# A hybrid decoder step: decayed scores over the later halves' columns, and one decayed tile per level in place of two

## The chip, the cores and the metric

The kernel runs on one core of a Trainium2 chip. Time is the device time of one launch in microseconds, the median of several runs. The engines are TensorE (PE, with its weight loads shown as PEld), VectorE (DVE), ScalarE (ACT), GpSimd (POOL) and the queues that move data.

## The reference

Two decoder layers run over 256 prompt tokens and 8 x 8 sample tokens. Each layer adds a mixer and then a feed-forward part (a dense SwiGLU in layer 0, the best two of eight experts in layer 1). The mixer projects to an HGRN2 group (4 heads, keys and values of 128) and a Mamba-2 group. The change touches the HGRN2 group alone:

```python
q, k, v, logf                  # (tokens, 4, 128); logf is the log of the forget gate
S_t = diag(f_t) S_{t-1} + k_t v_t^T          # per head
o_t = S_t^T q_t
# in chunks:
G      = cumsum(logf)
scores[t, s] = sum_k q[t, k] * exp(G[t, k] - G[s, k]) * k_in[s, k]    for s <= t
o_intra = scores @ v
o_inter = (q * exp(G)) @ state
```

The decay differs for each of the 128 components of a key, so the scores are no plain product of queries with keys: exp(G[t] - G[s]) has to be split at a token between s and t.

## The kernel before

**The levels.** The kernel splits a tile of 128 tokens in seven levels (LV = 7; in the tile of 64 sample tokens, sequences of 8, there are three, LS = 3). At level v the tokens are cut into blocks of 2b, b = 2^v, and each block into an earlier and a later half. A pair (s, t) belongs to the one level at which s lies in the earlier and t in the later half of one block, and its decay is split at the middle of that block: M[level v] holds, for every token, the decay between it and the middle of its block. So keys times M and queries times M, multiplied with each other, give the decayed scores of level v. A last level holds the pairs s = t. M is laid out with the 128 components on the partitions and (level, token) on the columns; M[nl] is the decay from the start of the tile.

**Tiles and heads.** TILES holds the tiles 0 and 1 (prompt, 128 tokens) and 2 (sample, 64 tokens); ORDER = (2, 0, 1), so HEADS, the list of pairs (tile, head) that the head loop runs over, has 12 entries per layer: four sample heads, four of the first prompt tile, four of the second. The loop runs once in each layer. Buffers alternate by head: M, Yq, Yk and SC have two copies each.

**The steps of a head.**
- exponents (PE, L1872): logs of the gates times a 0/1 table give the exponents of all levels in PSUM, in four products of 512 columns (two of 256 in the sample tile). ScalarE turns them into M ("decays", L800 and L803).
- products (VectorE, L1229): Yq = M times qT and Yk = M times kT, each one instruction over all levels (L1241, L1251). Between them stand, in the second prompt tile, qGp and egp (L1245, L1246) and, in the sample tile, egl and qG.
- scores (PE, L1887): for the levels 0 to 4 (LOW = 5) one product each of the whole tile, Yk by Yq (L1901); one of kT by qT for s = t (L1904); for the levels 5 and 6 only the blocks that are wanted, 2 + 1 products (L1908), into the columns of the last one. The tile's scores take 6 x 128 columns in two PSUM banks; the sample tile's 4 x 64.
- masked (VectorE, L1253): all of them times a 0/1 table into SC (L1260; L1263 in the sample tile).
- output (PE, L1913): the values (vtk) by each level's part of SC, six products that add up in one PSUM region (L1923; four in the sample tile), and in the second prompt tile one with the state (L1928).

All of it is fp32, and each fp32 product is two records in the trace. In a PE record `128*128 128x64` reads: the weights have 128 rows and 128 columns, the moving operand 128 rows and 64 columns.

**What sets the order.** PE's order is written out by hand at L2103 and below. For head j it issues: exponents of head j + 1; transposes and questions to the states of the sample sequences (turn_said, ask) where it is their turn; output of head j - 1; a piece of the sample's state; transposes of the values where a tile begins; scores of head j; transposes of the keys; the tile's state. At the last head of a tile the output stands ahead of the exponents. VectorE runs products of head j + 1, then masked of head j, then other pieces of the loop: the low half of the weights that come in for the next projection (spL, L1050, 2.3 us each), copies of states (SH), and so on. The engines keep in step by counters: y_done2 (products are ready), sc_mm (scores are in PSUM), sc_done (masked), o_mm (output read SC), x_exp (M is there). Before, scores of head j wait for sc_done of head j - 1, since all heads write the same two banks of scores.

## Time and profile before

| what | value |
|---|---|
| median of 3 runs | 1766.98 us (1762.48 to 1768.28) |
| the profiled execution | 1768.81 us, its span 1767.0 us |
| mean granted PE clock in it | 0.977 of full speed |
| PE busy | 1704.7 us, 96% |
| VectorE busy | 1291.5 us, 73% |
| ScalarE busy | 1039.1 us, 59% |
| GpSimd busy | 98.3 us, 6% |
| chain of work that ended last | PE 92%, DVE 5%, ACT 1%, issue 1% |

The profile is of one execution; its time stands 1.8 us above the median of the runs. Of a PE or VectorE row in a timeline the first number is the start and the second the length, both in us, "x9" says that nine like instructions follow each other, and brackets hold the idle time just before the row and what ended it. In the table of stretches each row is a stretch of the span, its length, then the busy time and, in brackets, the number of instructions of PE, PEld, DVE, ACT and POOL, the granted PE clock (1.00 is 2.4 GHz, 0.50 is 1.2 GHz), the share of the DMA engines and GB/s. Rows of groups give line, engine, operation, tiles, shapes and count, then total busy us and mean ns of one, then the idle time before them.

### The profile page before, as it was taken

Reading aid. Unit: us, or ns where it says so; the run is one execution under the profiler, and the core shown is the slowest. Engines: PE = TensorE matmul, PEld = TensorE weight load, DVE = VectorE, ACT = ScalarE, POOL = GpSimd, SP = SyncE. Lnnn points to the kernel's source line nnn. Section 1 sums busy time; section 2 is a strip of 40 time slices with the busy share of each in tenths; the row PEclk is TensorE's granted clock in tenths of the full one; section 3 lists DMA queues with packets and bytes.
Section 4 is the critical chain, followed back from the end, with each engine's and each line's share of the span. In section 5 each row is a group of like instructions: output and inputs, shape, how many; then the busy total and the mean of one; then the engine's idle time right before and its main releaser. Section 6 shows DMA issues by size and latency. Waiting matters only on the chain.

```text
span 1767.0 us, 23227 instructions
## 1 busy us (share of the span) xinstructions
PE 1704.7 (96%) x9594; PEld 1484.4 (84%) x9594; DVE 1291.5 (73%) x1119; ACT 1039.1 (59%) x942; POOL 98.3 (6%) x85
## 2 busy tenths in 40 slices
PE   8999889999999999789999999999999999899997
PEld 7988778999999978678888888888888888788886
DVE  6636755444357347649988888888888888888897
ACT  4443333333334344257777777777777777777776
POOL 2001120000000011203200000000000000000200
PEclk9997989999999989899999999999999999999999
DMA  9549263443553513259999999999999999899994
GB/s 298 167 149 276 57 180 109 160 141 102 146 168 123 164 39 85 60 179 341 392 394 396 397 366 388 367 387 394 363 386 377 366 398 386 312 394 365 381 393 186
DMA packets 272616, 474.07 MB, mean 268 GB/s; under 512 B 41578, under 2 KB 103266, under 8 KB 272504
## 3 DMA queue, kind: packets, MB, share of 16 engines
q1 hardware_dynamic: 266432, 452.37, 71.9%
q10 hardware_dynamic: 3368, 12.75, 2.2%
q0 software_dynamic: 2704, 7.39, 1.5%
q8 instruction: 78, 1.28, 0.3%
q14 instruction: 34, 0.28, 0.0%
HBM read 454.69 MB, written 29.84 MB: 274 GB/s over the span
## 4 chain that ended last, share of the span: by engine, by line
PE 92%; DVE 5%; ACT 1%; issue 1%; DMA 0%; ACTq 0%; DVEq 0%
PE ps L1712 17%; PE ps L1713 17%; PE ps L2355 12%; PE ps L1707 9%; PE ps L1708 9%; PE ps L2376 6%; PE ps L1806 4%; PE ps L2241 3%; PE ps L1923 2%; PE ps L2259 1%; PE ps L2394 1%; PE ps L1901 1%; PE ps L2203 1%; DVE spL L1592 1%; PE ps L1883 1%
## 5 line engine op out<-in xcount | busy, mean ns | idle before, releaser
L1592 DVE TENSOR_TENSOR spL<-ring,spH 128x2048 fp32r<-128x2048 f32 x336 | 767.3, 2292 | 99.2 <-ACT spH L967 96.5
L967 ACT ACTIVATE spH<-ring 128x2048 fp32r<-128x2048 f32 x336 | 643.0, 1916 | 130.7 <-PE ps L2355 68.1
L1712 PE MATMUL ps<-spH,XH 128*128 128x512 f32 x896 | 353.7, 395 | 1.8 <-issue 1.8
L1713 PE MATMUL ps<-spH,XL 128*128 128x512 f32 x896 | 349.4, 390 | 0.0
L1050 DVE TENSOR_TENSOR spL<-ring,spH 128x2048 fp32r<-128x2048 f32 (+1 forms) x74 | 158.8, 2146 | 182.3 <-ACT spH L662 182.2
L1707 PE MATMUL ps<-hnH,spH 128*128 128x320 f32 x928 | 277.4, 313 | 4.0 <-DVE hnL L1065 2.2
L1708 PE MATMUL ps<-hnL,spH 128*128 128x320 f32 x928 | 275.7, 311 | 0.0
L662 ACT ACTIVATE spH<-ring 128x2048 fp32r<-128x2048 f32 (+1 forms) x74 | 133.4, 1803 | 187.7 <-PE ps L2241 73.6
L2355 PE MATMUL ps<-spL,XH 128*128 128x512 f32 x896 | 240.9, 390 | 2.3 <-issue 1.8
L2355 PEld LDWEIGHTS ps<-spL,XH 128*128 128x128 f32 x896 | 168.0, 188 | 39.0 <-issue 2.2
L1712 PEld LDWEIGHTS ps<-spH,XH 128*128 128x128 f32 x896 | 168.3, 188 | 35.9 <-issue 2.2
L1713 PEld LDWEIGHTS ps<-spH,XL 128*128 128x128 f32 x896 | 168.4, 188 | 33.9
L1707 PEld LDWEIGHTS ps<-hnH,spH 128*128 128x128 f32 x928 | 176.5, 190 | 7.4 <-issue 4.8
L1708 PEld LDWEIGHTS ps<-hnL,spH 128*128 128x128 f32 x928 | 176.5, 190 | 0.2
L1712 PE MATMUL ps<-spH,hTH 128*128 128x512 f32 x448 | 175.9, 393 | 0.0
L1713 PE MATMUL ps<-spH,hTL 128*128 128x512 f32 x448 | 175.0, 391 | 0.0
L2376 PE MATMUL ps<-spL,hTH 128*128 128x512 f32 x444 | 119.2, 390 | 0.0
L1712 PEld LDWEIGHTS ps<-spH,hTH 128*128 128x128 f32 x448 | 84.1, 188 | 17.6
L1713 PEld LDWEIGHTS ps<-spH,hTL 128*128 128x128 f32 x448 | 84.2, 188 | 17.5
L2376 PEld LDWEIGHTS ps<-spL,hTH 128*128 128x128 f32 x444 | 83.4, 188 | 17.9
L1806 PE MATMUL ps<-hnH,spL 128*128 128x320 f32 x448 | 70.3, 309 | 0.0
L991 ACT ACTIVATE hTH<-ps 128x512 fp32r<-128x512 f32 x56 | 33.5, 599 | 60.9 <-PE ps L2394 60.9
(365 smaller groups left out, 1797.3 us busy)
## 6 DMA issues: line engine op xcount, KB each, us to landing
ring<-in_w_exp_in_dram SPq DMA_DIRECT2D x224, 1024.0 KB, 8.3
ring<-in_w_exp_out_dram SPq DMA_DIRECT2D x112, 1024.0 KB, 7.9
ring<-in_w_in_dram SPq DMA_DIRECT2D x28, 1024.0 KB, 5.3
ring<-in_w_ffn_in_dram SPq DMA_DIRECT2D x22, 1024.0 KB, 5.1
token_rows<-token_rows ACTq DMA_DIRECT2D x1, 11776.0 KB, 40.6
ring<-in_w_ffn_out_dram SPq DMA_DIRECT2D x16, 704.0 KB, 4.6
ring<-in_w_out_dram SPq DMA_DIRECT2D x8, 1024.0 KB, 5.0
out_dram<-ring SPq DMA_DIRECT2D x32, 256.0 KB, 2.7
```

What stands on the lines that cost most here:

```text
L662: A(spH[:, u % 2, 0:n], raw(u, n), ACT.Copy).then_inc(S("hi_done"), 1)
L967: A(esplit(j)[0], src, ACT.Copy).then_inc(S("hi_done"), 1)
L1050: V.tensor_tensor(spL[:, u % 2, 0:n], raw(u, n), spH[:, u % 2, 0:n].bitcast(F32), ALU.subtract).then_inc(S("split_done"), 1)
L1592: V.tensor_tensor(lo, eslot(j)[0], hi.bitcast(F32), ALU.subtract).then_inc(S("split_done"), 1)
L1707: mm(out, w, x[0], start=start, stop=False)
L1708: return mm(out, w, x[1], start=False, stop=False)
L1712: mm(out, x[0], w, start=start, stop=False)
L1713: return mm(out, x[1], w, start=False, stop=False)
L1806: m = mm(ps[:, 4 * (c % 2) + i, 0:TOK], wL[:, k, i * P:(i + 1) * P], hnH[:, kk], start=False, stop=kk == KT - 1)
L2241: m = mm(ps[:, 4 * (j % 2) + 2 * half + i, 0:TOK], wL[:, k, i * P:(i + 1) * P], hnH[:, k], start=False, stop=k == KT - 1)
L2355: m = mm(ps[:, 2 * (c % 2) + i // 2, :], XH[:, kk, xs], wL[:, k], start=False, stop=kk == KT - 1)
L2376: m = mm(ps[:, 6 + q, :], tH[:, f], wL[:, k, 512 * q:512 * q + 512], start=False, stop=c == EC - 1 and f == 3)
```

## The change

Four things are changed, and the number of PE's products in the loop is the same.

1. A token is only ever a key (earlier half) or a query (later half) of a level, never both. Yq and Yk become one tile Y: at level v the earlier halves of the blocks hold M times keys, the later ones M times queries. For that kT and qT become two halves of one buffer kq, and keys_then_queries describes, for one level, the columns of kq that alternate between keys and queries in runs of b. That description has one instruction per level, so two instructions of 7 x 128 columns become seven of 128 (two of 3 x 64 become three of 64). qGp or qG now stands ahead of them.
2. scores: the moving operand at the levels 0 to 4 is the later halves of Y only, 64 of 128 columns (32 of 64 in the sample tile). The weights are the whole of Y, so the number of weight columns stays. The results are packed: 5 x 64 + 128 = 448 columns in place of 768 (3 x 32 + 64 = 160 in place of 256), which fit in one bank. The head's parity now chooses the bank, and the scores wait for sc_done of the head before the last.
3. masked: one instruction over 448 (160) columns, with tables cut in the same way.
4. output: the product with the pairs s = t (and levels 5 and 6) comes first, over all columns; then each of the levels 0 to 4 adds to the columns of its later halves only, which in PSUM lie in runs of b with gaps of b (function later).

```diff
--- before.py
+++ after.py
@@ -87,7 +87,9 @@
     parts = {
         "w": wp.reshape(P, -1), "l": lp, "ws": ws.reshape(NS, -1), "ls": lspad,
         "id": np.eye(P), "ones": np.ones((P, P)),
-        "mask": np.concatenate([mp[:, :LOW], mp[:, LOW:].sum(1, keepdims=True)], 1).reshape(P, -1), "ms": ms.reshape(NS, -1), "seq": seq, "turn": turn,
+        "mask": np.concatenate([mp[:, v, (i >> v) % 2 == 1] for v in range(LOW)] + [mp[:, LOW:].sum(1)], 1),
+        "ms": np.concatenate([ms[:, v, (i[:NS] >> v) % 2 == 1] for v in range(LS)] + [ms[:, LS]], 1),
+        "seq": seq, "turn": turn,
         "iota": np.tile(i[None, :], (P, 1)), "before": (i[:, None] < i[None, :]),
     }
     at, n = {}, 0
@@ -220,8 +222,8 @@
 
 
         cursor[0] = arena
-        qT = put("qT", [P, H, TOK])
-        kT = put("kT", [P, H, TOK])
+        kq = put("kq", [P, 2, H, TOK])
+        kT, qT = kq[:, 0], kq[:, 1]
         lfT = put("lfT", [P, H, TOK])
         oT = put("oT", [P, H, TOK])
         ogT = put("ogT", [P, H, TOK])
@@ -243,8 +245,8 @@
         kdm = put("kdm", [NS, 4, H * P])
         ov = cursor[0]
         M = put("M", [P, LV + 1, P])
-        Yq = put("Yq", [P, LV + 1, P])
-        Yk = put("Yk", [P, LV, P])
+        Y = put("Y", [P, LV, P])
+        cursor[0] += 4 * 1024 + 512
         sc0 = cursor[0]
         SC = put("SC", [P, LV + 1, P])
         qG = put("qG", [P, H, NS])
@@ -265,8 +267,7 @@
 
         hn0 = base + 4 * KT * TOK
         Mb = [M, put("M1", [P, LV + 1, P], offset=hn0)]
-        Yqb = [Yq, put("Yq1", [P, LV + 1, P], offset=hn0 + 4 * 1024)]
-        Ykb = [Yk, put("Yk1", [P, LV, P], offset=hn0 + 8 * 1024)]
+        Yb = [Y, put("Y1", [P, LV, P], offset=hn0 + 4 * 1024)]
         SCb = [SC, put("SC1", [P, LV + 1, P], offset=hn0 + 11 * 1024 + 512)]
         ea = put("ea", [P, NSQ * NH], offset=hn0 + 15 * 1024 + 512)
         am = put("am", [P, NSQ, NH], offset=hn0 + 15 * 1024 + 768)
@@ -1226,19 +1227,21 @@
                     dve.wait_ge(S("k_tr"), i + 1)
                     V.tensor_tensor(kd_of(t)[0:n], kd_of(t)[0:n], ps[0:n, 7, :], ALU.mult).then_inc(S("kd_done"), 1)
 
+                def keys_then_queries(h, o, n, b):
+
+                    x = kq[:, 0, h, o:o + n]
+                    return bass.AP(tensor=x.tensor, offset=x.offset,
+                                   ap=[list(x.ap[0]), [2 * b, n // (2 * b)], [H * TOK + b, 2], [1, b]])
+
                 def products(t, h):
 
                     (o, n), j, nl = TILES[t], LTH(l, t, h), LV if t < 2 else LS
                     Mv = flat(Mb[h % 2])[:, 0:(nl + 1) * n].rearrange("p (v n) -> p v n", n=n)
-                    Yqv = flat(Yqb[h % 2])[:, 0:(nl + 1) * n].rearrange("p (v n) -> p v n", n=n)
-                    Ykv = flat(Ykb[h % 2])[:, 0:nl * n].rearrange("p (v n) -> p v n", n=n)
+                    Yv = flat(Yb[h % 2])[:, 0:nl * n].rearrange("p (v n) -> p v n", n=n)
                     dve.wait_ge(S("x_exp"), j + 1)
                     if j >= 2:
 
                         dve.wait_ge(S("sc_mm"), j - 1)
-                    q_b = qT[:, h, o:o + n].unsqueeze(1).broadcast_to([P, nl, n])
-                    k_b = kT[:, h, o:o + n].unsqueeze(1).broadcast_to([P, nl, n])
-                    V.tensor_tensor(Yqv[:, 0:nl], Mv[:, 0:nl], q_b, ALU.mult)
                     if t == 1:
                         if l and h == 0:
                             dve.wait_ge(S("ssp_stored"), 16 * l)
@@ -1248,20 +1251,21 @@
                         own(V.tensor_copy(egl[:, h], Mv[:, nl, LSQ - 1:n:LSQ]))
                         V.tensor_tensor(qG[:, h], Mv[:, nl], qT[:, h, o:o + n], ALU.mult
                                         ).then_inc(S("qG_done"), 1)
-                    V.tensor_tensor(Ykv, Mv[:, 0:nl], k_b, ALU.mult).then_inc(S("y_done2"), 1)
+                    for v in range(nl):
+                        b = 1 << v
+                        ins = V.tensor_tensor(Yv[:, v].rearrange("p (g r b) -> p g r b", r=2, b=b),
+                                              Mv[:, v].rearrange("p (g r b) -> p g r b", r=2, b=b),
+                                              keys_then_queries(h, o, n, b), ALU.mult)
+                    ins.then_inc(S("y_done2"), 1)
 
                 def masked(t, h):
                     n, j, nl = TILES[t][1], LTH(l, t, h), LV if t < 2 else LS
                     dve.wait_ge(S("sc_mm"), j + 1)
                     if j >= 2:
                         dve.wait_ge(S("o_mm"), j - 1)
-                    SCv = flat(SCb[h % 2])[:, 0:((LOW if t < 2 else nl) + 1) * n]
-                    if t < 2:
-                        V.tensor_tensor(SCv, ps[:, 2:4, :].rearrange("p b n -> p (b n)")[:, 0:(LOW + 1) * n], tabv("mask"),
-                                        ALU.mult).then_inc(S("sc_done"), 1)
-                    else:
-                        V.tensor_tensor(SCv[0:n], ps[0:n, 2, 0:(nl + 1) * n], tabv("ms")[0:n], ALU.mult
-                                        ).then_inc(S("sc_done"), 1)
+                    w = (LOW if t < 2 else LS) * n // 2 + n
+                    V.tensor_tensor(flat(SCb[h % 2])[0:n, 0:w], ps[0:n, 2 + h % 2, 0:w],
+                                    tabv("mask" if t < 2 else "ms")[0:n], ALU.mult).then_inc(S("sc_done"), 1)
 
                 def step_gates(t):
                     n = TILES[t][1]
@@ -1884,30 +1888,32 @@
                         m = mm(out, lfL[0:n, h * P:(h + 1) * P], w, start=False, stop=True)
                     m.then_inc(S("x_mm"), 1)
 
+                def later(x, v):
+
+                    return x.rearrange("p (g r b) -> p g r b", r=2, b=1 << v)[:, :, 1]
+
                 def scores(t, h):
 
                     (o, n), j, nl = TILES[t], LTH(l, t, h), LV if t < 2 else LS
                     pe.wait_ge(S("y_done2"), j + 1)
                     if (t, h) == HEADS[0]:
                         pe.wait_ge(S("cso_done"), 2 * l + 2)
-                    if j:
-
-                        pe.wait_ge(S("sc_done"), j)
-                    full = LOW if t < 2 else nl
-                    for v in range(full + 1):
-                        at_ = (v * n) % 512
-                        out = ps[0:n, 2 + (v * n) // 512, at_:at_ + n]
-                        if v < full:
-                            m = mm(out, flat(Ykb[h % 2])[:, v * n:(v + 1) * n],
-                                   flat(Yqb[h % 2])[:, v * n:(v + 1) * n], start=True, stop=True)
-                        else:
-                            m = mm(out, kT[:, h, o:o + n], qT[:, h, o:o + n], start=True, stop=True)
+                    if j >= 2:
+
+                        pe.wait_ge(S("sc_done"), j - 1)
+                    full, bank = LOW if t < 2 else nl, 2 + h % 2
+                    for v in range(full):
+                        m = mm(ps[0:n, bank, v * n // 2:(v + 1) * n // 2].rearrange("p (g b) -> p g b", b=1 << v),
+                               flat(Yb[h % 2])[:, v * n:(v + 1) * n],
+                               later(flat(Yb[h % 2])[:, v * n:(v + 1) * n], v), start=True, stop=True)
+                    at_ = full * n // 2
+                    m = mm(ps[0:n, bank, at_:at_ + n], kT[:, h, o:o + n], qT[:, h, o:o + n], start=True, stop=True)
                     for v in range(full, nl):
                         b = 1 << v
                         for s0 in range(0, n, 2 * b):
-                            m = mm(ps[s0:s0 + b, 2 + (full * n) // 512, at_ + s0 + b:at_ + s0 + 2 * b],
-                                   flat(Ykb[h % 2])[:, v * n + s0:v * n + s0 + b],
-                                   flat(Yqb[h % 2])[:, v * n + s0 + b:v * n + s0 + 2 * b], start=True, stop=True)
+                            m = mm(ps[s0:s0 + b, bank, at_ + s0 + b:at_ + s0 + 2 * b],
+                                   flat(Yb[h % 2])[:, v * n + s0:v * n + s0 + b],
+                                   flat(Yb[h % 2])[:, v * n + s0 + b:v * n + s0 + 2 * b], start=True, stop=True)
                     m.then_inc(S("sc_mm"), 1)
 
                 def output(t, h):
@@ -1919,9 +1925,11 @@
                         pe.wait_ge(S("o_evac"), i)
                     out = ps[:, 6, h * n:(h + 1) * n]
                     top = LOW if t < 2 else nl
-                    for v in range(top + 1):
-                        m = mm(out, vtk_of(t)[0:n, h * P:(h + 1) * P], flat(SCb[h % 2])[0:n, v * n:(v + 1) * n],
-                               start=v == 0, stop=v == top and t != 1)
+                    vh, sc = vtk_of(t)[0:n, h * P:(h + 1) * P], flat(SCb[h % 2])[0:n]
+                    mm(out, vh, sc[:, top * n // 2:top * n // 2 + n], start=True, stop=False)
+                    for v in range(top):
+                        m = mm(later(out, v), vh, sc[:, v * n // 2:(v + 1) * n // 2].rearrange("p (g b) -> p g b", b=1 << v),
+                               start=False, stop=v == top - 1 and t != 1)
                     if t == 1:
                         if h == 0:
                             pe.wait_ge(S("sh_done"), 2 * l + 1)
```

**On VectorE**, in layer 0 where the first prompt tile's head 1 gives way to head 2, there stood (ps is PSUM, tab the tables, ring and spH the weights that come in):

```order
L1260 TENSOR_TENSOR SC_105<-ps,tab 128x768 [waits o_mm,sc_mm]
L1050 TENSOR_TENSOR spL<-ring,spH 128x2048 [waits hi_done]
L1360 COPY SH<-ps 128x512 [waits st_mm]
L1241 TENSOR_TENSOR Yq_103<-M_102,qT 128x896 [waits sc_mm,x_exp]
L1251 TENSOR_TENSOR Yk_104<-M_102,kT 128x896
L1260 TENSOR_TENSOR SC<-ps,tab 128x768 [waits o_mm,sc_mm]
```

and now:

```order
L1267 TENSOR_TENSOR SC_102<-ps,tab 128x448 [waits o_mm,sc_mm]
L1051 TENSOR_TENSOR spL<-ring,spH 128x2048 [waits hi_done]
L1364 COPY SH<-ps 128x512 [waits st_mm]
L1256 TENSOR_TENSOR Y_101<-M_100,kq 128x128 [waits sc_mm,x_exp]
L1256 TENSOR_TENSOR Y_101<-M_100,kq 128x128 x6
L1267 TENSOR_TENSOR SC<-ps,tab 128x448 [waits o_mm,sc_mm]
```

Nothing changed its place; two products became seven and the masks are narrower.

**On PE**, at the output of a prompt head of the first prompt tile and the scores that follow it (an order row counts products, not records), there stood:

```order
L1923 MATMUL ps<-SC,vtk 128x128 [waits o_evac,v_done,sc_done]
L1923 MATMUL ps<-SC,vtk 128x128 x5
L1901 MATMUL ps<-Yq_103,Yk_104 128x128 [waits sc_done,y_done2]
L1901 MATMUL ps<-Yq_103,Yk_104 128x128 x4
L1904 MATMUL ps<-qT,kT 128x128
L1908 MATMUL ps<-Yq_103,Yk_104 32x32 x2
L1908 MATMUL ps<-Yq_103,Yk_104 64x64
```

and now:

```order
L1929 MATMUL ps<-SC,vtk 128x128 [waits o_evac,v_done,sc_done]
L1931 MATMUL ps<-SC,vtk 128x64
L1931 MATMUL ps<-SC,vtk 128x32x2
L1931 MATMUL ps<-SC,vtk 128x16x4
L1931 MATMUL ps<-SC,vtk 128x8x8
L1931 MATMUL ps<-SC,vtk 128x4x16
L1906 MATMUL ps<-Y_101 128x64 [waits sc_done,y_done2]
L1906 MATMUL ps<-Y_101 128x64 x4
L1910 MATMUL ps<-kq 128x128
L1914 MATMUL ps<-Y_101 32x32 x2
L1914 MATMUL ps<-Y_101 64x64
```

Here too the places are the same; the products of the levels 0 to 4 are 64 columns wide, on both sides of the masks, and those of the output write stepped columns.

## Rows read from the trace of the kernel before

**Rows 1.** The page's head, busy time of each engine.

```profile
PE 1704.7 (96%) x9594; PEld 1484.4 (84%) x9594; DVE 1291.5 (73%) x1119; ACT 1039.1 (59%) x942; POOL 98.3 (6%) x85
```

**Rows 2.** Table of stretches; columns: stretch, length, five engines, clock, DMA, GB/s.

```profile
126.90:154.20 27.30, 26.85 (x118) 21.18 (x116) 11.19 (x26) 8.73 (x13) 6.19 (x4) 0.50 1.02 332
154.30:202.00 47.70, 46.10 (x450) 40.42 (x450) 36.76 (x55) 22.13 (x49) 2.88 (x3) 1.00 0.54 148
188.40:191.70 3.30, 2.75 (x32) 2.33 (x30) 1.99 (x5) 2.45 (x8) 0.00 (x0) 1.00 0.37 109
215.70:219.10 3.40, 3.40 (x44) 2.50 (x41) 3.37 (x6) 0.00 (x0) 0.00 (x0) 0.50 0.70 154
632.10:638.90 6.80, 6.51 (x49) 4.93 (x49) 4.75 (x16) 2.57 (x6) 2.28 (x3) 1.00 0.07 16
639.00:655.90 16.90, 16.45 (x71) 13.12 (x70) 6.36 (x11) 6.02 (x7) 3.90 (x3) 0.50 0.00 1
656.00:706.00 50.00, 48.39 (x470) 42.44 (x469) 38.86 (x59) 23.30 (x53) 5.01 (x4) 1.00 0.37 85
```

**Rows 3.** Timeline of PE, runs of like records: start, length, shapes, count.

```profile
158.29 1.17 PE L1901 MATMUL ps<-Yq,Yk 128*128 128x128 f32 x9
...
636.21 0.83 PE L1923 MATMUL ps<-SC,vtk 64*128 64x64 f32 x6
...
784.98 0.61 PE L2272 MATMUL ps<-sml,tab 128*128 128x8 f32 x4
...
634.11 0.56 PE L1901 MATMUL ps<-Yq,Yk 128*64 128x64 f32 x6
...
151.06 2.13 PE L1901 MATMUL ps<-Yq,Yk 128*128 128x128 f32 x9
...
139.81 1.70 PE L1923 MATMUL ps<-SC,vtk 64*128 64x64 f32 x7
```

**Rows 4.** Timeline of VectorE, around a prompt head's products and masks.

```profile
157.98 1.08 DVE L1241 TENSOR_TENSOR Yq<-M,qT 128x896 f32<-128x896 f32 x1
158.99 1.08 DVE L1251 TENSOR_TENSOR Yk<-M,kT 128x896 f32<-128x896 f32 x1
160.16 0.96 DVE L1260 TENSOR_TENSOR SC<-ps,tab 128x768 f32<-128x768 f32 x1
...
171.49 0.28 DVE L1245 TENSOR_TENSOR qGp<-M,qT 128x128 f32<-128x128 f32 x1
171.69 0.14 DVE L1246 COPY egp<-M 128x1 f32<-128x1 f32 x1
```

**Rows 5.** Groups of VectorE instructions, different shapes apart.

```profile
L1260 DVE TENSOR_TENSOR SC<-ps,tab 128x768 f32<-128x768 f32 x16 | 15.3, 957 | 22.1 <-PE ps L1908 22.0
...
L1263 DVE TENSOR_TENSOR SC<-ps,tab 64x256 f32<-64x256 f32 x8 | 3.3, 413 | 3.0 <-PE ps L1904 3.0
...
L1248 DVE COPY egl<-M 128x8 f32<-128x8 f32 x8 | 1.3, 162 | 0.0
L1246 DVE COPY egp<-M 128x1 f32<-128x1 f32 x8 | 1.2, 147 | 0.0
```

**Rows 6.** Timeline of PE, layer 0, around its waits for masks.

```profile
145.65 0.63 PE L1883 MATMUL ps<-tabR,lfH 128*128 128x512 f32 x1
146.07 0.63 PE L1884 MATMUL ps<-tabR,lfL 128*128 128x512 f32 x1
147.08 1.97 PE L1923 MATMUL ps<-SC,vtk 64*128 64x64 f32 x8 [0.38 <-DVE SC L1263]
...
165.20 0.51 PE L1908 MATMUL ps<-Yq,Yk 128*32 128x32 f32 x6
...
166.85 1.60 PE L1923 MATMUL ps<-SC,vtk 128*128 128x128 f32 x12 [0.55 <-DVE SC L1260]
...
192.20 1.60 PE L1923 MATMUL ps<-SC,vtk 128*128 128x128 f32 x12 [1.05 <-DVE SC L1260]
```

**Rows 7.** Timeline of PE, layer 1, an output of the sample tile.

```profile
635.93 1.10 PE L1923 MATMUL ps<-SC,vtk 64*128 64x64 f32 x8 [0.15 <-DVE SC L1263]
```

## The prediction

> **What bounds the kernel now.** I read the head of the page first: PE is busy for 96% of the span and VectorE for 73% [rows 1]. A change pays where it shortens PE's own queue or a wait of PE. The edits lie in one stage, the head loop of the two mixers: 12 heads per layer, about 126.6 to 202 us and 632 to 706 us. The table of stretches shows the reader two things there [rows 2]. PE has almost no gap: 46.1 of 47.7 us and 48.4 of 50.0 us busy in the later part of the two loops. And the loop runs at two clocks: the granted clock is 0.50 (1.2 GHz) from 126.9 to 154.2 us and from 639 to 656 us, and 1.00 (2.4 GHz) behind that.
>
> **What a narrower product costs on PE.** Each fp32 product is two records in the trace. In a run of back-to-back records the distance of two starts is (length of the run − length of its last record) / (records − 1); single records of these shapes last 0.22 to 0.28 us at 2.4 GHz and 0.42 at 1.2. At 2.4 GHz, by the lengths in [rows 3]:
> - 128 stationary and 128 moving columns: (1.17 − 0.275) / 8 = 0.112 us.
> - 128 stationary and 64 moving: (0.83 − 0.27) / 5 = 0.112 us.
> - 128 stationary and only 8 moving: (0.61 − 0.26) / 3 = 0.117 us, with a first gap that is longer.
> - 64 stationary and 64 moving: (0.56 − 0.22) / 5 = 0.07 us.
> At 1.2 GHz, with 0.42 us for one record, nine of 128 by 128 give (2.13 − 0.42) / 8 = 0.214 us and seven of 128 by 64 give (1.70 − 0.42) / 6 = 0.213 us.
> So the wider of the two operands sets the pace. The change halves only the moving one: score levels go from 128 by 128 to 128 by 64, the value products likewise, and in the sample tile from 64 by 64 to 64 by 32 and from 128 by 64 to 128 by 32. The stationary side stays, so I cost all of this at **0 on PE**. Their number stays too (10 + 2 + 6 score records and 12 output records per prompt head).
> The output products now write stepped columns of the accumulator; no row shows such a write. With 64 moving columns half of the 0.112 us is spare, so a write at half pace is hidden: 0 as the low end, and one more 0.112 us for each of the 10 stepped records as the high end, 1.1 us per prompt head, 17.9 us for 16. I take 0.
> The Trainium skill, SBUF — State Buffer, in its note on cachelines, says of the accumulator's 8-byte lines that "any non-contiguous PSUM access pattern significantly slows down matmuls". It speaks against this change, and no row here shows either side; by it the sum would move to the high end just named.
>
> **VectorE, products.** Before, two products of 896 elements run from 157.98 to 160.07 us, 2.09 us [rows 4]. Now seven of 128 elements. A 128-element product of the same tensors holds the engine for 171.69 − 171.49 = 0.20 us and ends 0.28 us after its start [rows 4], so 6 × 0.20 + 0.28 = 1.48 us: −0.61 us per prompt head. The new right operand jumps between keys and queries in runs of 1, 2, 4 elements. A copy of 8 elements 32 bytes apart takes 162 ns against 147 ns for one, 2.1 ns an element, where the masks below pay 1.06 ns an element [rows 5]. If all 128 elements cost the double, an instruction takes 0.2 + 0.14 = 0.34 us and the seven 2.4 us: +0.3 us. I take the low end, since out and left operand stay contiguous and five of seven levels have runs of 4 or more. Sample tile: 2 × 192 elements become 3 × 64, half the elements and one start more: −0.1 us.
> **VectorE, masks.** 768 columns take 957 ns and 256 take 413 ns [rows 5], 1.06 ns a column: 448 columns 617 ns (−0.34 us), 160 columns 311 ns (−0.10 us).
> Together VectorE sheds 16 × 0.95 + 8 × 0.2 = 17 us. Nearly all lies beside PE's work; only what PE waits for counts.
>
> **The waits of PE on these.** The chain shows them; layer 0, and the same three come in layer 1 [rows 6]:
> - 147.08 us: the last sample output waits for its mask, which stands behind both products of the next head. PE could go on at 146.50, one 512-wide record (146.07 − 145.65 = 0.42 us) behind 146.07. The new mask is ready 0.61 + 0.10 earlier, at 146.37: −0.58 us (with slow products +0.2).
> - 166.85 us: VectorE has no pause from its mask at 160.16 [rows 4]. That run gets 0.34 + 0.61 us shorter to the next mask, and then this mask waits for its scores, whose last record ends at 165.20 + 0.51 = 165.71; 0.04 + 0.62 + 0.04 later is 166.41: −0.44 us (with slow products −0.3).
> - 192.20 us: PE has nothing between the last but one scores and their output: −0.34 us.
> That is −1.36 us a layer. In layer 1 the first sample heads run at 2.4 GHz, and PE's wait of 0.15 us at 635.93 us goes, as does a smaller one in the head behind [rows 7]: −0.2 us. Sum: −2.7 − 0.2 = **−2.9 us** (with slow products about −0.9).
> The relaxed wait of the scores (the mask of the head before the last instead of the last) is worth 0: in PE's order the output of the last head stands ahead and waits for the same count. That qGp (and qG in the sample tile) now stands ahead of the products moves nothing, as its 0.2 us and the pause behind egp were there. The shorter tables are 0.2 MB less in a transfer that lands long before its use at 126 us.
>
> **The clock.** The rise at 154.2 us comes behind a stretch in which PE streamed 12 score records of 128 columns at 0.21 us each, between full-width transposes [rows 3]. Ahead of it, from 126.9 us on, PE was as busy (26.85 of 27.3 us [rows 2]) and the clock stayed low; what differs is that many of its records moved 64 columns where the weights took the time of 128. Layer 1 shows more: with PE busy for 6.5 of 6.8 us the clock fell at 639 us, in the middle of such records. The changed kernel makes the score records just ahead of the rise of that kind. So I expect no rise at 154 us. Behind them come, at 1.2 GHz, four transposes and four 512-wide exponents at 0.42 us [rows 6], and 32 question products with all columns moving; I expect the rise there, one low stretch of 3.4 us later, as the one at 215.7 us lasted [rows 2]. What is done in it takes twice its time: +1.7 us a layer, **+3.4 us**. The bounds are 0 and, if the clock stays low for 16 us more in a layer (to the next such run at 170 us), +8 us a layer.
>
> **Sum.** 1768.8 (the profiled execution; its span is 1767.0) − 2.9 + 3.4 = 1769.3. That execution stood 1.8 above the median of the runs, so the median goes to 1767.0 + 0.5, **1767.5 us**. Runs of before spread by 5.8 us; a difference under 0.3% (5.3 us) can't be told from none.
>
> **Rivals.**
> - *The clock is not touched.* For it: PE's busy share stays as it is. Against: 639 us, above. 1767.0 − 2.9 = **1764**.
> - *Half the columns is half the time.* The 20 level records of a prompt head go from 0.112 to 0.056 us: 1.12 us × 16 = 17.9, with the 2.9: **1746**. Against it stand the runs with 64 and 8 moving columns, whose pace is that of 128. For it only that most of them contract over 64 rows. The Trainium skill, TensorE: Matmul & The Clock Gate, in its section on the back-to-back issue gap, gives the gap of a single product by its moving columns alone and would have it so; the rows with 64 moving columns contradict it for fp32 weights.
> - *Slower: the clock falls again or stays low.* In the second prompt tile a head consists of output, state and score products; with half of their columns gone the stretch at 188.4 us, which is already the thinnest but for its waits [rows 2], is where it would fall, and it would come back at the questions at 204 us. 16 us at half clock are +8 us a layer: **1775.5** if in one layer, 1783.5 in both. It decides if the clock reads below 1.00 anywhere from 158 to 204 us or 660 to 706 us.
> - *Slower: stepped writes cost a second pass.* 17.9 us more: **1785**. It decides from the point at which a stepped record takes over 0.112 us.
>
> **How the numbers follow.** Forecast 0.50 (1767.5). Clock untouched 0.20 (1764). Columns pay 0.07 (1746). Clock falls or stays low 0.17 (1775.5 to 1783.5). Stepped writes 0.06 (1785). Low end 1761: the 1764 less half of the runs' spread; high end 1778, to include the clock loss in one layer with its spread. Left out are 0.07, 0.06 and some 0.07 of the clock's. Faster than 1761.7: 0.07 and a seventh of the second case, 0.10. Slower than 1772.3: 0.06 + 0.15, 0.21. Within: 0.69.
>
> **What would show it.** The distance of output and score records at 2.4 GHz, still 0.112 us. Lengths of the new products 0.28 us at a pitch of 0.20, of the masks 0.62 and 0.31 us. PE's waits on the masks of 1.0 to 1.3 us gone but for about 0.7 at the last one. The clock's rise near 157.7 and 659 us, and 1.00 from there to 215 and 717. I am wrong if the level records lie closer than 0.11 us, if stepped ones lie farther apart, or if the clock rises at 154 as before.

## The result

The changed kernel takes 1773.13 us (median of 11 runs, 1769.24 to 1777.75), the kernel before 1767.18 us (median of 11, 1761.88 to 1770.82). The ratio is 1.004, 95% interval [1.0029, 1.0051]: slower by about 6 us. The forecast was 1767.5 us in a range of 1761 to 1778. The time lies inside the range, but not for a reason that the prediction gave.

The profiled execution of the changed kernel took 1771.83 us, its span is 1769.9 us. The head of its page answers [rows 1]:

```profile
span 1769.9 us, 23314 instructions
...
PE 1710.1 (97%) x9594; PEld 1483.4 (84%) x9594; DVE 1276.6 (72%) x1207; ACT 1039.1 (59%) x942; POOL 96.2 (5%) x85
```

PE runs the same 9594 records; VectorE works 14.9 us less (17 were expected), with 88 instructions more.

**The head loops.** The timeline of PE around the rise in layer 0 and at the waits (start, length, shapes, count, idle time before):

```profile
145.91 2.23 PE L1906 MATMUL ps<-Y 128*128 128x64 f32 x10
...
152.02 1.78 PE L1968 MATMUL ps<-ring,qG 128*32 128x128 f32 x32
153.74 0.49 PE L1929 MATMUL ps<-SC,vtk 128*128 128x128 f32 x2
154.06 1.23 PE L1931 MATMUL ps<-SC,vtk 128*128 128x64 f32 x10
155.13 1.28 PE L1906 MATMUL ps<-Y 128*128 128x64 f32 x10
...
163.43 0.49 PE L1929 MATMUL ps<-SC,vtk 128*128 128x128 f32 x2
...
188.27 0.49 PE L1929 MATMUL ps<-SC,vtk 128*128 128x128 f32 x2 [0.72 <-DVE SC L1267]
```

The ten score records of 64 moving columns start at 155.13 and the next product at 156.24: 0.111 us each. The ten stepped output records take (155.13 − 154.06) / 10 = 0.107 us. Neither the halved columns nor the stepped writes change the pace of PE. The wait of 0.55 us on a mask at 166.85 us [rows 6] is no longer listed, the one of 1.05 us is 0.72.

VectorE, the groups with forms apart (total us, mean ns) and one prompt head's products in the timeline:

```profile
L1267 DVE TENSOR_TENSOR SC<-ps,tab 128x448 f32<-128x448 f32 x16 | 10.0, 625 | 32.5 <-PE ps L1914 32.5
...
L1267 DVE TENSOR_TENSOR SC<-ps,tab 64x160 f32<-64x160 f32 x8 | 2.5, 313 | 0.9 <-PE ps L1910 0.9
```

```profile
167.45 1.53 DVE L1256 TENSOR_TENSOR Y<-M,kq 128x128 f32<-128x128 f32 x7
```

The table of stretches answers [rows 2]: the low stretch of layer 0, the rest of that loop, the low stretch of layer 1, and then a stretch far behind, in the experts:

```profile
133.04:153.52 20.48, 20.41 (x106) 16.26 (x108) 8.74 (x27) 7.41 (x9) 3.97 (x3) 0.50 1.00 323
153.60:201.00 47.40, 46.55 (x458) 41.43 (x454) 30.07 (x86) 22.66 (x52) 3.73 (x4) 1.00 0.57 154
...
634.90:655.20 20.30, 20.23 (x104) 16.14 (x108) 8.60 (x26) 7.38 (x9) 3.82 (x3) 0.50 0.01 3
...
793.10:1489.90 696.80, 694.10 (x3121) 568.70 (x3120) 620.05 (x370) 519.59 (x353) 26.38 (x9) 1.00 1.02 380
```

The same 3120 records of the experts in the kernel before, from its own table:

```profile
797.10:1488.60 691.50, 688.80 (x3121) 568.70 (x3120) 620.03 (x370) 519.44 (x353) 26.10 (x9) 1.00 1.02 383
```

This is the finding of the comparison. When the experts begin, the changed kernel is 4.0 us ahead (793.1 against 797.1 us). Over the next 691.5 us it loses 5.3 us, at the full clock, with the same records, the same work on the other engines and the same traffic; to the last of the expert records it loses 6.6 us. The loss grows evenly: 0.7 us after 100 us, 2.3 after 300, 4.7 after 600. The diff touches no line of that stage. From 255 to 626 us, in layer 0's dense feed-forward part, the two kernels keep step to 0.01 us. The groups of PE records in the two stretches show where: first before, then after.

```profile
L1712 PE MATMUL ps<-spH,XH 128*128 128x512 f32 x657 | 259.1, 394 | 0.0
...
L1712 PE MATMUL ps<-spH,hTH 128*128 128x512 f32 x320 | 125.5, 392 | 0.0
```

```profile
L1716 PE MATMUL ps<-spH,XH 128*128 128x512 f32 x657 | 260.7, 397 | 0.0
...
L1716 PE MATMUL ps<-spH,hTH 128*128 128x512 f32 x320 | 126.7, 396 | 0.0
```

The records of these two groups are 3 to 4 ns longer, while those with XL and hTL in the place of XH and hTH keep their 390 and 391 ns, and no wait appears. What the diff does change for this stage is where its buffers lie. `put` hands out addresses one behind the other; the mask tables are 416 columns narrower, so everything behind the tables (from `arena` on) moved down by 4 x 416 = 1664 bytes, the slots ring6, spH2 and spL2 for incoming weights and the sums sg, hTH and hTL among them. The buffers ahead of the tables (ring, spH, spL, XH, XL) did not move.

### The profile page after: what moved, and what is told of

Read it like the earlier page. It is cut to its first block, busy times and chain, and to the rows that moved or that the text cites. A ratio compares the mean times of both kernels' runs of the same rounds, so it can differ in the third digit from the quotient of the medians.

```text
span 1769.9 us, 23314 instructions
## 1 busy us (share of the span) xinstructions
PE 1710.1 (97%) x9594; PEld 1483.4 (84%) x9594; DVE 1276.6 (72%) x1207; ACT 1039.1 (59%) x942; POOL 96.2 (5%) x85
## 4 chain that ended last, share of the span: by engine, by line
PE 94%; DVE 4%; ACT 1%; issue 1%; DMA 0%; ACTq 0%; DVEq 0%
PE ps L1716 17%; PE ps L1717 17%; PE ps L2363 12%; PE ps L1711 9%; PE ps L1712 9%; PE ps L2384 6%; PE ps L1810 4%; PE ps L2249 3%; PE ps L1931 1%; PE ps L2267 1%; PE ps L1906 1%; PE ps L2402 1%; PE ps L2211 1%; PE ps L1887 1%; PE ps L1968 1%
```

## The experiments

Two questions: does the address cost the 6 us, and is the rest of the sum (waits saved, clock lost) right? Since all kernels run the same 9594 PE records in nearly the same order, the start of the same record can be compared in each. Five stretches are enough:

- **R0, R1**: from the last transpose record of the keys of the first prompt head to the next state product, layer 0 (in the kernel before 154.59 to 160.72 us), and from the same record to that head's output, layer 1 (656.36 to 659.82). Whether the clock has risen by then decides their length.
- **T0, T1**: from there through the rest of the loop to a record of the SSD stage behind it (160.72 to 211.81 us, 659.82 to 709.69).
- **X**: 3120 records of the experts (797.14 to 1488.61 us).

| kernel | R0 | R1 | T0 | T1 | X | low clock, layer 0 / 1 |
|---|---|---|---|---|---|---|
| before | 6.13 | 3.46 | 51.09 | 49.87 | 691.47 | 27.3 / 17.1 |
| after | 7.75 | 5.18 | 50.16 | 48.99 | 696.81 | 20.5 / 20.5 |
| e1 before again | 6.13 | 3.47 | 51.10 | 49.84 | 691.33 | 20.5 / 10.2 |
| e2 after, old addresses | 7.65 | 5.15 | 50.13 | 48.96 | 691.47 | 30.7 / 20.5 |
| e3 before, +384 bytes | 6.13 | 3.47 | 51.10 | 49.88 | 696.68 | 17.1 / 17.1 |
| e4 both halved | 7.72 | 4.51 | 57.25 | 56.09 | 691.45 | 30.7 / 20.5 |
| e5 after, three slots back | 7.65 | 5.14 | 50.17 | 48.97 | 692.95 | 30.7 / 20.5 |
| e6 tile Y only | 6.13 | 3.47 | 51.00 | 49.77 | 691.52 | 27.3 / 10.2 |
| e7 scores halved | 7.35 | 5.06 | 51.09 | 49.86 | 691.51 | 30.7 / 20.5 |
| e8 output halved | 6.12 | 3.40 | 51.09 | 49.90 | 691.46 | 27.3 / 17.1 |
| e9 before, +256 bytes | 6.12 | 3.47 | 51.08 | 49.86 | 691.38 | 10.2 / 10.2 |
| e10 before, +512 bytes | 6.12 | 3.47 | 51.09 | 49.84 | 691.37 | 10.2 / 10.2 |
| e11 Y and both halved | 7.69 | 4.86 | 57.15 | 55.93 | 691.43 | 30.7 / 20.5 |
| e12 wide scores, old addresses | 6.13 | 3.41 | 50.21 | 49.04 | 691.43 | 27.3 / 6.8 |

The last column is the time that the clock read 0.50 in the head loops up to its rise.

**e1, the kernel before once more.** No edit.

> The kernel before once more, unchanged, for a second profile of it. It tells what in the head loop of layer 0 is the kernel and what is the moment at which the clock is looked at. In the first profile PE's clock fell at 126.9 us, in the changed kernel's at 133.0 us, though both do the same work up to there. Theory: where it falls is set by where the kernel happens to stand, not by the change; then this profile may show the fall up to 3.4 us away from 126.9 or at 133, and the span differs by up to 3 us from 1767. Rival: the fall belongs to the kernel; it stays within 0.5 us of 126.9. Both: ratio 1.000 +- 0.001, the expert stage (from the first of its 896 products of L1712 on) as in the first profile: 907.5 us between 797.1 and 1704.7.

Measured: 1766.24 us, ratio 1.0 [0.9984, 1.0017]. The clock fell at 124.57 us, rose at 141.63 and was low once more from 145.05 to 148.46:

```profile
124.57:141.63 17.06, 17.06 (x80) 13.41 (x78) 6.68 (x21) 4.09 (x8) 6.21 (x4) 0.50 1.02 333
145.05:148.46 3.41, 3.41 (x15) 2.99 (x15) 1.25 (x2) 1.69 (x4) 0.00 (x0) 0.50 1.02 293
```

The fall is 2.3 us from 126.9, so the rival falls by its own mark; but all of this execution stands 2.56 us earlier, and counted from the PE record at 116.6 us (114.02 here) the clock fell 10.3 and 10.6 us later, at nearly the same record. What differs between these two executions of one program is how long the clock stayed low ahead of the first prompt head: 27.3 and 20.5 us. The low time in layer 0 was 27.3, 20.5, 17.1 and 10.2 us in kernels whose order of PE records there is that of before. So the 3.9 us that the profiled execution of the changed kernel gained in layer 0 (134.6 us against 138.4 us between the records that start at 116.6 and 255.0 us in the kernel before) are no gain of the change: e3, with the code of before, shows 134.7, and e2, with the code of after, 138.5. The later fall (16.5 to 16.9 us behind that record) came in the profiles of the changed kernel, e3, e9 and e10, the four in which the slots ring6, spH2 and spL2 stand elsewhere, and in none of the ten others. With one profile each, a link isn't shown; the medians speak against a steady gain, since e3 takes 7.3 us more than the kernel before and its profile loses 6.7 us in the experts alone.

**e2, the changed kernel with the old addresses.**

```diff
+        cursor[0] += 4 * 416
         arena = cursor[0]
```

> The changed kernel, with one edit: the buffers behind the tables start where they started before (1664 bytes higher; the narrower masks had moved all of them down). Theory A, layout: the loss of 6.6 us in the stage of the experts (907.5 to 914.2 us for the same PE records) comes from the moved addresses. Then the stage returns to 907.5 us and the ratio to the kernel before is 0.9965 to 0.999 (1761 to 1765 us). Rival B: it comes from something else in the program or the run; the stage stays at 914 us and the ratio at 1.003 to 1.005. The head loops are as in the changed kernel under both.

Measured: 1766.76 us against 1765.92, ratio 1.0002 [0.999, 1.0013]. Its experts:

```profile
795.61:1487.08 691.47, 688.77 (x3122) 568.72 (x3121) 620.11 (x370) 519.40 (x353) 26.16 (x9) 1.00 1.03 382
```

The stage is back at the pace of before to the hundredth of a microsecond, and 6 us of the median are gone. The total is above what was expected (0.9965 to 0.999; it took the short layer 0 of one profile for a gain), and the interval only touches that range. The address costs the loss, and everything else in the change sums to nothing that can be measured.

**e3, the kernel before with the addresses 384 bytes up.** The counter-test: none of the change but the place within 2048 bytes.

```diff
+        cursor[0] += 384
         arena = cursor[0]
```

> The kernel before, with the buffers behind the tables 384 bytes higher: the same place within 2048 bytes as in the changed kernel (1664 + 384 = 2048). Theory A with the address within 2048 bytes as what counts: the stage of the experts takes 914 us, ratio 1.003 to 1.005. Theory A with another property (only the distance to one neighbour, or a larger period): something between 907 and 914 us. Rival B: 907.5 us, ratio 1.000. The head loops are those of before.

Measured: 1773.22 us, ratio 1.0036 [1.002, 1.0052], X = 696.68 us:

```profile
791.20:1487.88 696.68, 693.97 (x3121) 568.59 (x3120) 620.13 (x370) 519.69 (x353) 24.25 (x9) 1.00 1.02 380
```

The kernel before has become as slow as the changed one, by one line that moves buffers. Rival B falls.

**e5, three slots at their old place in the changed kernel.**

```diff
+        cursor[0] += 4 * 416
         ring6 = put("ring6", [P, 1, UN])
```

> The changed kernel with only the last three buffers of the experts' stage (ring6, spH2, spL2: one of the slots each for incoming weights and their halves) back at the addresses that they had before; all others behind the tables (sums, gates, hTH, hTL) stay 1664 bytes lower. What is known: all of them back gives 1766.8 us, none 1773.1. Theory: the place of the weight slots counts, since in the kernel before all slots stand at the same place within 512 bytes (128) and in the changed one these three do not; then the stage of the experts takes 907.5 us and the median is 1766 to 1768. Rival: hTH, hTL or sg count; the stage stays at 914 us and the median at 1772 to 1774. In between if both do.

Measured: 1768.39 us, ratio 1.0018 [0.9999, 1.0038], X = 692.95 us. The slots ring6, spH2 and spL2 carry 3.9 of the 5.3 us (696.81 − 692.95); the 1.5 us left belong to what still stands 1664 bytes lower. In the groups of that run the records with hTH are still long, those with XH are not:

```profile
L1717 PE MATMUL ps<-spH,XH 128*128 128x512 f32 x657 | 259.2, 394 | 0.0
...
L1717 PE MATMUL ps<-spH,hTH 128*128 128x512 f32 x320 | 126.5, 395 | 0.0
```

**e9 and e10, the period.** The kernel before with 256 and with 512 bytes in place of the 384 of e3.

> The kernel before with the buffers behind the tables 256 bytes higher; read is the length of the stage of the experts (907.5 us before, 914.2 us with 384 bytes more). In the kernel before ring, spH, spL, XH and XL and the last three slots all stand at 128 within 512 bytes; with 256 more the moved ones stand at 384. If the place within 256 bytes counts, the stage takes 907.5 us; if it is the place within 512 bytes or more, 909 to 915 us.

> The kernel before with the buffers behind the tables 512 bytes higher. If the place within 512 bytes (or less) counts, the stage of the experts takes 907.5 us as before; if it is a larger period, or any move away from the old place, 909 to 915 us.

One profiled execution each (1762.69 and 1758.79 us; single times, which say nothing about the kernels). The experts:

```profile
786.57:1477.95 691.38, 688.68 (x3122) 568.66 (x3121) 620.10 (x370) 519.43 (x353) 26.11 (x9) 1.00 1.02 383
```

```profile
786.79:1478.15 691.36, 688.63 (x3121) 568.72 (x3120) 620.09 (x370) 519.46 (x353) 26.13 (x9) 1.00 1.02 382
```

Moves of 256 and 512 bytes are free in this stretch; moves of 384 and of −1664 bytes, which are odd multiples of 128, cost 5.2 and 5.3 us. That fits a place within 256 bytes as what counts. It isn't shown, since the two costly moves are the same place within 2048 bytes (1664 + 384 = 2048) and no move of 128 or 640 bytes was run. By the offsets that `put` hands out, all weight slots and XH, XL stand at one place within 256 bytes in the kernel before; in the changed kernel the three moved slots stand 128 bytes from it. (The stage as a whole took 911.4 us in e9, since the clock was low twice behind the records of X, at 1504.9 and 1511.7 us; X itself lies ahead of that.) Why the place matters (which of PE's reads, of the conversions' writes or of the transfers get in each other's way) isn't told apart by these runs. Nor was one buffer alone moved.

**e4, PE's halves alone.** The kernel before, with only the operands of the level products halved:

```diff
-                            m = mm(out, flat(Ykb[h % 2])[:, v * n:(v + 1) * n],
-                                   flat(Yqb[h % 2])[:, v * n:(v + 1) * n], start=True, stop=True)
+                            m = mm(later(out, v), flat(Ykb[h % 2])[:, v * n:(v + 1) * n],
+                                   later(flat(Yqb[h % 2])[:, v * n:(v + 1) * n], v), start=True, stop=True)
...
+                    mm(out, vh, sc[:, top * n:(top + 1) * n], start=True, stop=False)
+                    for v in range(top):
+                        m = mm(later(out, v), vh, later(sc[:, v * n:(v + 1) * n], v),
+                               start=False, stop=v == top - 1 and t != 1)
```

> The kernel before, with only PE's operands halved: the level products of the scores and of the output move the later halves' columns (64 in place of 128), read from Yq and SC with steps and written to PSUM with steps; the same result, the layout, the tables, VectorE's products and masks stay as before. Theory: the pace of these records stays 0.112 us at 2.4 GHz (the 128 weight columns set it), and the clock in both layers rises 3.4 us later than before, which costs 2 us a layer, with no waits on masks saved: ratio 1.000 to 1.003, near 1771 us. Rival (clock untouched by the columns): rise at 154 and 656 us, ratio 1.000. Rival (columns pay): 1747 us. Rival (stepped columns cost): the level records are over 0.12 us apart, 1780 us or more.

Measured: 1780.8 us, ratio 1.0084 [1.0065, 1.0103], slower than the theory had it (near 1771 us). By the time alone it would be the rival of stepped columns (1780 us or more), but that rival's sign, records over 0.12 us apart, isn't there (below). The rise came later, as the theory had it (R0 7.72, R1 4.51). But the clock fell a second time, in both layers, in the tile and at the place of the prediction's slower rival:

```profile
193.94:207.60 13.66, 13.66 (x75) 12.13 (x75) 4.60 (x11) 3.59 (x12) 3.96 (x4) 0.50 0.24 70
702.53:716.18 13.65, 13.65 (x71) 12.09 (x70) 4.41 (x8) 3.59 (x12) 3.96 (x4) 0.50 0.27 77
```

The loop behind the rise took 57.25 us in place of 51.09, and 56.09 in place of 49.87: +6.2 us a layer. The records themselves kept their pace: ten output records of 64 columns with stepped reads and writes from 192.43 us on end in the same 1.23 us.

```profile
192.11 0.49 PE L1927 MATMUL ps<-SC,vtk 128*128 128x128 f32 x2 [1.05 <-DVE SC L1260]
192.43 1.23 PE L1929 MATMUL ps<-SC,vtk 128*128 128x64 f32 x10
```

**e7 and e8, one half each.** The first of the two edits of e4, and the second.

> The kernel before; only the level products of the scores move the later halves' 64 columns in place of 128. What is known: with both scores and output halved, and nothing else changed, the clock fell a second time, at 193.9 to 207.6 and 702.5 to 716.2 us, and the time was 1780.8 us. Theory: each half is a step to that fall, the scores have 10 records a head and the output 10; with one of them alone the clock stays up behind its rise, and only the rise in front moves back by 3.4 us where the scores are those just ahead of it: 1768 to 1771 us. Rival: the scores alone bring the second fall: 1778 to 1781 us.

> The kernel before; only the level products of the output move 64 columns in place of 128 and write stepped columns. Theory: the clock rises as before (ahead of the rise at 154 and 656 us stand scores, not outputs of a prompt head) and stays up: ratio 1.000, 1765 to 1768 us. Rival: the output alone brings the second fall at about 190 us, in the tile whose heads have output, state and scores only: 1774 to 1780 us. Stepped writes: if they cost, these records alone are more than 0.112 us apart.

Measured: e7 1772.13 us, ratio 1.0048 [1.0028, 1.0068]; e8 1769.59 us, ratio 1.0029 [1.0008, 1.005]. The scores alone move the rise (R0 7.35, R1 5.06), the output alone doesn't (6.12, 3.40). Neither brings the second fall (T0 51.09 in both). e7 took 1 us more than expected. Its profiled execution, 3.5 us above its median, shows one thing more: the low stretch of the SSD stage behind the loop, 3.4 us long in the kernel before [rows 2], is 6.8 us.

```profile
214.13:220.96 6.83, 5.85 (x53) 4.70 (x54) 5.76 (x11) 0.00 (x0) 0.00 (x0) 0.50 0.36 79
```

In layer 0, e1, the kernel before, has 6.8 us there too (209.9 to 216.7), so this can't be booked on the edit.

e8 was expected at 1765 to 1768 and its profiled loop is that of before. Its ten runs still show a mean clock of 0.975 (median of runs; 0.979 in the runs of before beside them). Where other executions lose it isn't seen; this stays open.

**e6, VectorE's tile Y alone.** keys_then_queries and one Y, PE 128 columns wide, masks 768 wide, old addresses.

```diff
-                    V.tensor_tensor(Yqv[:, 0:nl], Mv[:, 0:nl], q_b, ALU.mult)
...
-                    V.tensor_tensor(Ykv, Mv[:, 0:nl], k_b, ALU.mult).then_inc(S("y_done2"), 1)
+                    for v in range(nl):
+                        b = 1 << v
+                        ins = V.tensor_tensor(Yv[:, v].rearrange("p (g r b) -> p g r b", r=2, b=b),
+                                              Mv[:, v].rearrange("p (g r b) -> p g r b", r=2, b=b),
+                                              keys_then_queries(h, o, n, b), ALU.mult)
+                    ins.then_inc(S("y_done2"), 1)
```

> The kernel before with VectorE's part of the products alone: one tile Y, by the token's place keys or queries times the decays, in seven instructions a prompt head. PE's records stay 128 columns wide, masks stay 768 wide, the layout of the rest stays. [...] Ratio 0.998 to 1.000, near 1765 us. Rival (VectorE's steps cost the double): no gain, ratio 1.000 to 1.001. Rival (the clock falls again with less work on VectorE): it cannot, PE's records are the same; a second fall between 158 and 205 us would overturn the theory on columns.

Measured: 1762.82 us against 1765.2, ratio 0.9992 [0.9973, 1.0011]: no difference that can be told. T0 and T1 are 0.1 us shorter than before, R0 and R1 the same, no second fall. Beside e2 (T0 50.13) this says that the products alone carry little of the saving behind the rise, 0.1 of 0.9 us a layer. The rest needs what e6 leaves out; the narrow masks come with the packed scores, the one bank and the relaxed wait, and these were not run apart.

**e11, tile Y with both halves.** e6 with the edits of e4; masks still 768 wide.

> The kernel before with the one tile Y on VectorE (0.5 us less a prompt head) and PE's level products of scores and output halved; masks still 768 columns, two banks, layout as before. What is known: halved with the old VectorE work the clock fell a second time (193.9 to 207.6 us, 702.5 to 716.2) and took 1780.8 us; with all of VectorE's savings it did not, and took 1766.8 us. Theory: the second fall comes where PE moves few columns and waits for masks besides; the waits for the masks at the heads of the last tile are still there (1.0 us at 192 us, since the mask alone sets it), so the fall comes: 1776 to 1781 us, low from about 193 to 207 us. Rival: the products' part is enough to prevent it: 1766 to 1769 us.

Measured: 1781.21 us, ratio 1.0093 [1.0067, 1.012]. The second fall is there (T0 57.15, T1 55.93), and so is the wait of 1.05 us for the mask just ahead of it:

```profile
195.91:209.57 13.66, 13.66 (x76) 12.13 (x77) 4.67 (x11) 3.59 (x12) 3.96 (x4) 0.50 0.24 68
```

```profile
194.00 0.49 PE L1934 MATMUL ps<-SC,vtk 128*128 128x128 f32 x2 [1.05 <-DVE SC L1267]
```

What e2 has and e11 hasn't is the narrow mask, the packed scores in one bank and the wait relaxed by a head; with them the wait is 0.72 us and no second fall comes in any of the three profiles (after, e2, e5). That the shorter wait is what keeps the clock up fits all five profiles with halved scores and output, but the three were not taken apart.

**e12, the scores wide again.** The changed kernel at the old addresses; each score product moves its 64 later columns twice, and the next product writes over the second copy. Same result, same packed layout, same masks.

```diff
+                def twice(x, v):
+                    b, n = 1 << v, x.shape[1]
+                    return bass.AP(tensor=x.tensor, offset=x.offset + b,
+                                   ap=[list(x.ap[0]), [0, 2], [2 * b, n // (2 * b)], [1, b]])
...
-                        m = mm(ps[0:n, bank, v * n // 2:(v + 1) * n // 2].rearrange("p (g b) -> p g b", b=1 << v),
+                        m = mm(ps[0:n, bank, v * n // 2:v * n // 2 + n].rearrange("p (c g b) -> p c g b", c=2, b=1 << v),
                                flat(Yb[h % 2])[:, v * n:(v + 1) * n],
-                               later(flat(Yb[h % 2])[:, v * n:(v + 1) * n], v), start=True, stop=True)
+                               twice(flat(Yb[h % 2])[:, v * n:(v + 1) * n], v), start=True, stop=True)
```

> The changed kernel with the buffers behind the tables at their old place, and the level products of the scores move the 64 later columns twice (the second copy lands where the next product writes over it): 128 columns a record again, with the packed results and the narrow masks of the change. Theory: a record still takes 0.112 us, since the 128 weight columns set it, so this costs nothing, and the clock rises in both layers one look earlier than in the changed kernel, which gives back 1.7 to 2 us a layer: ratio 0.997 to 0.999, 1760 to 1764 us, faster than both. Rival (the columns have nothing to do with the rise): as with the layout alone, ratio 1.000, 1766 us. Rival (the columns do cost): 1770 us or more.

Measured: 1761.45 us against 1763.88, ratio 0.9992 [0.9976, 1.0009]. The mechanism is as expected: double the columns at no cost, and the clock rises ahead of the exponents again (R0 6.13, R1 3.41), with the savings of the masks kept (T0 50.21, T1 49.04).

```profile
147.10 2.34 PE L1913 MATMUL ps<-Y 128*128 128x128 f32 x10
...
151.19 0.48 PE L1888 MATMUL ps<-tabR,lfH 128*128 128x512 f32 x1
151.51 0.39 PE L1889 MATMUL ps<-tabR,lfL 128*128 128x512 f32 x1
```

```profile
151.16:157.29 6.13, 6.13 (x73) 5.25 (x73) 4.83 (x12) 3.31 (x3) 0.00 (x0) 1.00 1.00 340
```

The mean clock of its runs is 0.979 (median; 0.980 in the runs of before beside them), of e2's 0.975 (0.978 beside them). The size is less than hoped: no difference from the kernel before is shown, and the interval also holds the ratio of e2. No version was shown to beat the kernel before.

## Why the prediction was right, and where it wasn't

- **Pace of PE**: right. 0.111 us a score record and 0.107 us a stepped output record, against 0.112 us before. Both rivals of that part (columns pay, stepped writes cost) fall. The Trainium skill, SBUF — State Buffer, in its note on cachelines, says that any non-contiguous access to PSUM slows matmuls significantly; here stepped writes in runs of 1 to 16 fp32 cost no time. As the prediction says, a write at half the pace would be hidden beside 64 moving columns, and no run has a stepped write 128 columns wide, so whether the write itself is slower isn't shown. The Trainium skill, TensorE: Matmul & The Clock Gate, in its section on the back-to-back issue gap, gives the gap by the moving columns for an isolated product; of a stream of weight loads and products it says that both set the spacing, which the prediction left out. The trace agrees with the latter: with fp32 weights of 128 columns the gap doesn't fall with the moving columns from 128 to 64.
- **VectorE**: right. Seven products in 1.53 us (1.48 expected), masks of 625 and 313 ns (617 and 311). In sum it shed 14.9 us, where 17 were expected.
- **Waits**: right, a little low. Behind the rise a layer gains 0.93 and 0.88 us (T0, T1) where 0.78 was expected. In layer 1 the part ahead of the rise went from 26.15 to 25.28 us, 0.87 us where 0.78 was expected.
- **Clock**: right in mechanism and size for the rise. It comes behind the transposes and exponents, and R0 and R1 are longer by 1.6 and 1.7 us (1.7 expected a layer). Undone by e12, brought about by the scores alone in e7. The sign has to be read by records, though: the prediction would be wrong "if the clock rises at 154 as before", and it rose at 153.5 and 655.3 us, since that execution stood 4 to 5 us earlier there. Against the record that opens R0 and R1 the rise came 3.5 and 3.8 us later, and in the kernel before 0.3 and 0.4 us earlier. The low stretch of layer 1 was 20.5 us in all six kernels with narrow scores and 6.8 to 17.1 us in the eight with wide ones, so some executions lose more than those 3.4 us of low clock; the prediction had that only as a bound.
- **The sum**: +0.5 us was expected; e2, which is the change without its addresses, shows a ratio of 1.0002 [0.999, 1.0013], +0.8 us between medians. Layer 1, where the profiles of before and after fall alike, gives 83.88 against 83.91 us.
- **The slower rival** (the clock falls again) did not happen in the changed kernel, but e4 and e11 show it at its place and at 6.2 us a layer, where 8 was worked out. What fits these runs is that the waits for masks decide it; the prediction asked for fewer columns only. That wasn't separated from the packed scores and the relaxed wait, so the cause stays open.
- **The step that failed** is one sentence: "The shorter tables are 0.2 MB less in a transfer that lands long before its use at 126 us." It took the shorter tables for a transfer alone. They also move every buffer behind them by 1664 bytes, and that costs 6 us in a stage that the diff doesn't touch. That the range held is luck in part: it was made wide for the clock, and the 6 us came from elsewhere. The same goes for the 0.21 given to a time above 1772.3 us, where the time fell. A step that asked where `put` places what comes behind the tables would have found the move, though nothing in the profile of before gives its price.

## What to carry to other kernels

An edit that changes the size of a table moves all buffers behind it. Compare the addresses of the hot buffers before and after, and time the change once with padding that keeps them in place: otherwise the time of the layout is booked on the edit. And of two operands of an fp32 product ask which one sets the pace before the other is narrowed; narrowing the cheap one saves nothing and can cost the clock.

## What the runs showed of the hardware

- The place of SBUF buffers is worth 0.77% of a stage that is bound by PE while ScalarE and VectorE convert incoming weights: 696.8 and 696.7 us against 691.3 to 691.5 us for the same records. Moves by 256 and 512 bytes cost nothing (691.38, 691.37), moves by 384 and −1664 bytes 5.2 and 5.3 us.
- A PE that is busy for 13.66 of 13.66 us with narrow records can stand at 0.50, as at 193.94 us in e4 and 195.91 in e11; in e2, with records as narrow and a wait of 0.72 us ahead of them in place of 1.05, it kept 1.00. That the wait is the cause isn't shown.
- Ten fp32 records with 128 weight columns take 1.1 us at 2.4 GHz with 64 moving columns or with 128, and with 64 also where they are written to PSUM in steps.
